# Unused bytes behind feed-forward tiles and weight slots in a two-block transformer kernel

## What is computed

```python
def swiglu(x, w_gate, w_up, w_down):
    return (jax.nn.silu(x @ w_gate) * (x @ w_up)) @ w_down

def first_block(x, ...):
    xn = rmsnorm(h, g_mix[l])
    z = xn @ w_in[l] + b_in[l]                    # a convolution and a pooling branch follow
    h = h + jnp.concatenate([y_conv, y_pool], axis=-1) @ w_out[l]
    h = h + swiglu(rmsnorm(h, g_ffn[l]), w_gate[l], w_up[l], w_down[l])
    return rmsnorm(h, g_final)

def second_block(x, ...):
    for layer in range(2):
        h = _fox_attention(...) if layer == 0 else _diff_attention(...)
        x = _layer_norm(DN_ALPHA * x + h, ...)
        f = _conv_ffn(x, ...)                     # x @ w_in, taps, silu(g) * val, @ w_out
        x = _layer_norm(DN_ALPHA * x + f, ...)
    return x
```

## Time and profile before

| What | Value |
| --- | --- |
| median of 3 executions | 1816.34 us (1816.28 to 1817.22) |
| the profiled execution, first to last instruction (its span; no other time of it is given) | 1818.9 us |
| PE busy | 1774.2 us (98%), 8755 matmuls |
| POOL busy | 1029.9 us (57%) |
| ACT busy | 795.8 us (44%) |
| DVE busy | 765.2 us (42%) |

### The profile page before, as it was taken

The page is one execution under the profiler, slowest core; times in us unless marked ns, Lnnn a source line. Parts: engine busy times, 40 slices in busy tenths (PEclk is TensorE's granted clock), DMA queues, the critical chain, the costliest instruction groups (busy, mean ns, idle before and its releaser), DMA issues.

```text
span 1818.9 us, 26859 instructions
## 1 busy us (share of the span) xinstructions
PE 1774.2 (98%) x8755; PEld 1477.6 (81%) x8755; DVE 765.2 (42%) x1382; ACT 795.8 (44%) x1674; POOL 1029.9 (57%) x926
## 2 busy tenths in 40 slices
PE   8999999999999999999999999999999999999997
PEld 6879888888887888788888888877777888888886
DVE  7963000001235556553333322487875533333224
ACT  5644323322245555464444422555565644444231
POOL 7856555555462333466666655555554666666551
PEclk9999999999999999999999999999999999999999
DMA  5312333323334454323333233333332233332332
GB/s 153 92 47 82 104 92 92 101 87 103 91 90 115 123 133 122 86 73 99 102 92 94 85 104 87 82 94 81 87 77 79 63 111 93 96 100 78 104 91 97
DMA packets 327253, 171.94 MB, mean 95 GB/s; under 512 B 43459, under 2 KB 316949, under 8 KB 327189
## 3 DMA queue, kind: packets, MB, share of 16 engines
q1 hardware_dynamic: 327172, 171.12, 33.8%
q10 hardware_dynamic: 16, 0.00, 0.0%
HBM read 152.15 MB, written 2.10 MB: 85 GB/s over the span
## 4 chain that ended last, share of the span: by engine, by line
PE 87%; DVE 5%; POOL 3%; ACT 2%; issue 1%; DMA 1%; SPq 0%; DVEq 0%; ACTq 0%; POOLq 0%
PE bank L982 24%; PE bank L984 24%; PE bank L983 24%; PE attended L982 2%; PE attended L983 2%; PE attended L984 2%; PE turned L1423 1%; POOL WL L741 1%; PE attended L1439 1%; PE bank L1055 1%; PE bank L1067 1%; POOL psums L804 1%; PE bank L1068 1%; DVE small L2453 0%; PE score L1406 0%
## 5 line engine op out<-in xcount | busy, mean ns | idle before, releaser
L741 POOL TENSOR_TENSOR WL<-raw,WH 128x512 fp32r<-128x512 f32 (+3 forms) x656 | 774.8, 1203 | 555.6 <-ACT WH L1604 553.1
L982 PE MATMUL bank<-XL,WH 128*128 128x512 f32 x1432 | 568.8, 397 | 3.7 <-DVE work L2576 1.2
L984 PE MATMUL bank<-XH,WL 128*128 128x512 f32 x1432 | 557.8, 390 | 0.0
L983 PE MATMUL bank<-XH,WH 128*128 128x512 f32 x1432 | 557.4, 389 | 0.0
L1604 ACT ACTIVATE WH<-raw 128x512 fp32r<-128x512 f32 (+3 forms) x656 | 338.5, 565 | 307.7 <-PE bank L984 190.9
L984 PEld LDWEIGHTS bank<-XH,WL 128*128 128x128 f32 x1432 | 269.7, 188 | 56.8
L982 PEld LDWEIGHTS bank<-XL,WH 128*128 128x128 f32 x1432 | 270.1, 189 | 55.6 <-DVE work L2576 1.5
L983 PEld LDWEIGHTS bank<-XH,WH 128*128 128x128 f32 x1432 | 270.4, 189 | 49.9
L982 PE MATMUL bank<-HL,WH 128*128 128x512 f32 (+1 forms) x528 | 200.6, 380 | 0.0
L983 PE MATMUL bank<-HH,WH 128*128 128x512 f32 (+1 forms) x528 | 200.3, 379 | 0.0
L984 PE MATMUL bank<-HH,WL 128*128 128x512 f32 (+1 forms) x528 | 200.3, 379 | 0.0
(11 more groups left out here) (366 smaller groups left out, 2532.0 us busy)
## 6 DMA issues: line engine op xcount, KB each, us to landing
raw<-in_ffn_w_in SPq DMA_DIRECT2D x88, 512.0 KB, 3.8
raw<-in_w_gate SPq DMA_DIRECT2D x22, 512.0 KB, 3.8
raw<-in_w_up SPq DMA_DIRECT2D x22, 512.0 KB, 3.9
raw<-in_ffn_w_out SPq DMA_DIRECT2D x28, 384.0 KB, 3.3
raw<-in_ffn_w_out SPq DMA_DIRECT2D x28, 320.0 KB, 3.2
raw<-in_a_w_in SPq DMA_DIRECT2D x16, 512.0 KB, 4.2
raw<-in_kv_w SPq DMA_DIRECT2D x32, 256.0 KB, 3.2
raw<-in_w_in SPq DMA_DIRECT2D x12, 512.0 KB, 3.8
```

The lines of the kernel that those rows point to most:

```text
L741: pool.tensor_tensor(wl, x, wh, ALU.subtract).then_inc(w_lo, 1)
L982: pe.matmul(out_, wh, xl, start=start, stop=False)
L983: pe.matmul(out_, wh, xh, start=False, stop=False)
L984: return pe.matmul(out_, wl, xh, start=False, stop=stop)
```

## The change

Every tile of `HH` and `HL` and every slot of `WH` gets 64 unused bytes behind it, every slot of `WL` 32. The views that the rest of the code uses leave the unused bytes out, so nothing else in the code differs. The instructions on all five engines are the same ones in the same order; no wait, no DMA and no size is changed.

```diff
-        WH = sb("WH", [P, SLOTS, DT, P], F32R)
-        WL = sb("WL", [P, SLOTS, DT, P], F32R)
+        WH = sb("WH", [P, SLOTS, DT * P + 16], F32R)[:, :, 0:DT * P].rearrange("p s (k c) -> p s k c", k=DT)
+        WL = sb("WL", [P, SLOTS, DT * P + 8], F32R)[:, :, 0:DT * P].rearrange("p s (k c) -> p s k c", k=DT)
...
-        HH = sb("HH", [P, FT, S], F32R, stack=ffn)
-        HL = sb("HL", [P, FT, S], F32R, stack=ffn)
+        HH = sb("HH", [P, FT, S + 16], F32R, stack=ffn)[:, :, 0:S]
+        HL = sb("HL", [P, FT, S + 16], F32R, stack=ffn)[:, :, 0:S]
```

## The result

The changed kernel takes 1823.89 us (median of 6 runs, 1821.4 to 1825.76), the kernel before 1816.62 us (1815.61 to 1817.22). The ratio is 1.0039, with a 95% interval from 1.0029 to 1.005: 7 us slower, between 5.3 and 9.1.

The account below looks back on a forecast made before the run. PE, busy 98%, was taken to bound the kernel by number of matmuls times their distance. Terms 7.5 + 7.5 - 4.7 - 0.6 - 0.1 = +9.6 us on 1816.3 gave 1825.9, say 1826 us, range 1808 to 1837.5.

Parts of the forecast that it names:

- the step of 6.8 ns that goes with addresses: 512-column matmuls: 226.5 ns with X (moving tile and weights at one residue modulo 256), 233.3 with H and O (tile 64 lower).
- Weight slots under X: X matmuls of 512 columns: +7.5 us from known offset -64, plus +7.5 us as middle of 0 to +15.1 for unseen offsets.
- The sign that the prediction asked for: X stretch: slot 0 stays at 226.5 ns, slot 1 takes about 233 for two of three matmuls.
- the offsets without a row: X weight slots at offsets 128, 64, -32 and -96, unseen in the trace: 2220 matmuls priced between nothing and 6.8 ns.
- `head_gates`: Nearest row, moving operand at 128, weights at all four residues: 232.1 ns; by it three moved slots pay 18.6 us, not 15.0.
- Feed-forward tiles: 1386 H matmuls of 512 columns: offsets spread evenly, half the 6.8 ns price gone, -4.7 us, ends -2.4 and -7.1.
- O, forecast -0.6 us: O tiles move from 64 to 192 against slots at four residues: half the price gone, -0.6 us, ends -0.3 and -0.9.
- 256 columns: Sides swapped: 396 H matmuls lose, +1.3 us; three quarters of 576 X matmuls can gain, -1.4 us; together -0.1 us.
- The other engines: ACT and POOL writing to new residues: taken as 0, with 3 us up or down as a bound.
- The moving tile's own address: Faster rival, chance 0.26: the weights' address is free, X keeps 226.5 ns, H gains; 1811.6 us, or 1808 to 1814.
- No change: Rival, chance 0.17: addresses have no part, X differs from H and O in something that stays; 1816.3 us.
- Any offset but 0 costs the whole step: Slower rival, chance 0.12: 3330 X matmuls pay 6.8 ns, +22.6 us, H gains only its quarter, -2.4; 1836.5 us.

## Why the prediction was right, step by step

*What bounds the kernel, and the step of 6.8 ns that goes with addresses:* right. The step is 233.3 - 226.7 = 6.6 ns (the 6.8 had the rounding of the start times in it), and ten kernels moved distances by moving buffers alone.

*Weight slots under X, forecast +15.0 us:* right in sign, somewhat too large. By slots the distances rose by 0.8, 4.6, 3.7 and 2.5 ns over 226.7; times 1110 matmuls each this is 12.9 us at the price of an undisturbed stretch, and 10.4 us over the whole trace (below). The sign that the prediction asked for, about 233 ns for two of three matmuls in slot 1, came true. A row tile there in the changed kernel:

```profile
868.75 0.40 PE L982 MATMUL bank<-XL,WH 128*128 128x512 f32 x1
868.98 0.39 PE L983 MATMUL bank<-XH,WH 128*128 128x512 f32 x1
869.22 0.39 PE L984 MATMUL bank<-XH,WL 128*128 128x512 f32 x1
869.44 0.40 PE L982 MATMUL bank<-XL,WH 128*128 128x512 f32 x1
```

Over nine such items the two matmuls with `WH` (offset -64) take 235.8 and 231.6 ns, 233.7 in the mean. But the one with `WL` (offset -32) takes 226.8, as before, though -32 alone costs the whole step. What the sum had wrong is that each load pays the steady price of its own offset: by the steady prices slot 1 would take 233.3 ns and slot 2 232.8 (two loads at 232.5, one at 233.3), and they take 231.3 and 230.4. So that the middle came near is partly luck. Of the offsets without a row 128 (232.5) and -32 (233.3) turned out dear and 64 cheap (228.9), -96 was not tried, and the mixing took part of it back. `head_gates` at 232.1 ns, which I kept for the range, would have overstated it.

*Feed-forward tiles, forecast -4.7 us:* mis-sized. H fell by 1.9 ns, not by 3.4: 1386 x 1.9 = -2.6 us. Two things were wrong in the working: of the two offsets not shown one (128) is nearly as dear as -64, and a run in which the offset changes from matmul to matmul need not take the mean of the steady prices, (226.7 + 233.3 + 232.5 + 228.9) / 4 = 230.4 ns: with padded tiles it takes more, 231.4 and 231.7, with the slots alone 230.5.

*O, forecast -0.6 us:* 186 x 3.7 ns = -0.7 us in the stretch shown.

*256 columns, forecast +1.3 and -1.4 us:* H rose from 113.3 to 117.9 ns, 396 x 4.6 = +1.8 us; X fell from 120.0 to 117.9, 576 x 2.1 = -1.2 us.

*The other engines, forecast 0:* right as far as waits show it. PE's longest waits are 9.1 and 4.8 us where they were 9.3 and 5.1, and POOL's busy time rose by 5 us of 1030 without a wait of PE behind it.

The terms as measured add up to 12.9 - 2.6 - 0.7 + 1.8 - 1.2 = +10.2 us, and the time rose by 7.3, between 5.3 and 9.1. The two traces show where most of the rest went. Both hold 8755 matmuls in the same order, so that their distances can be compared one by one. X of 512 columns rose by 2.9 ns a matmul in the stretches without waits (949 matmuls in 815 to 1030 us of the trace before, 882 in 1470 to 1670), but by 2.0 and 1.1 ns in the two stretches with attention (528 each, 535 to 755 and 1165 to 1400 us), and in the first 120 us its 336 did not rise. Its sum is +10.4 us, not 12.9. H's is -2.6, as above. So the full price was paid where matmuls follow each other undisturbed; that the waits between attention work took up the rest is only argued. These are sums over one profile of each kernel, and those two executions differ by 4.4 us.

That the forecast of +9.6 us lies 2.3 from the result is partly luck: the loss of X was taken 2.1 to 4.6 us too large and the gain of H 2.1 us too large, and the two cancel.

*The rivals.* "The moving tile's own address" is refuted by the kernel with weights 64 bytes higher: tiles that did not move got slow, tiles that moved to 128 stayed slow. "No change" is refuted by the same run, and with it what the prediction drew from the two read ports of the Trainium skill ("SBUF — State Buffer", section "Who interferes with whom"), that an address could not matter: the distance between two matmuls depends on the two addresses together, 226.7 or 233.3 ns. Whether the ports themselves are independent no run here shows. "Any offset but 0 costs the whole step" was nearer than I gave it credit for: -64, -32, -16, 32 and 128 cost all or nearly all of it when every load has the same one. It fails at 64, which costs a third, and in runs in which the offset changes, as in the changed kernel, whose 1823.9 us are far from its 1836.5.

## What to carry to other kernels

Where matmuls follow each other without a gap, look at the distance between their starts and not at their busy time, and compare families that do the same work: here a fixed difference of a few nanoseconds hung on the addresses of their operands and was paid thousands of times. Before spreading buffers over addresses, work out at which relation they lie now. Here three quarters of the work sat at the best one, by accident, and spreading could only lose it for them; 64 bytes in one place, which bring the rest to the same relation, gained about 5 us.

## What the runs showed of the hardware

For matmuls of 512 float32 columns with 128 weight columns, at the 2.4 GHz level, the distance from start to start depended on the difference between the address of the moving tile and that of the weights, modulo 256 bytes (128 bytes changed it, 256 did not). In undisturbed stretches where every load had the same difference it was 226.7 ns at 0, 228.9 at 64, 232.5 at 128 and 233.3 at -64, -32, -16 and 32. It did not depend on the address itself, as far as tried: at -64 it was 233.3 with the moving tile at 0, 64, 128 and 192, and at 0 it was 226.7 with both at 128 and both at 192. With 256 columns the order is the other way: 120.0 ns at 0, 113.3 at -64. I had not expected that 16 bytes cost as much as 64, nor that one load of three at another offset costs two thirds of the step (231.1 ns), and that a matmul at offset 0 then takes 228.3 or 229.3 ns beside it. Prices of mixed offsets could not be worked out from the steady ones: they came out above the mean there, and below it in slots 1 and 2 of the changed kernel (231.3 and 230.4 ns). What in the chip makes the two addresses meet is not visible in the trace, which shows starts and ends of instructions only; that reads of the moving tile and of the next weights get in each other's way would fit, and is not shown.
